# Moving a softplus series, splitting a recurrence around a product, and leaving the last chunk of four output tiles to the end

## The reference

```python
z = x @ w_in                               # 8 x 512 mixer columns, then 4 x 1024 gate columns
# A: RG-LRU
a_conv = causal_dwconv(rg_buf, a_x, rg_conv_w) + rg_conv_b
r = sigmoid(a_conv @ w_a + b_a); i = sigmoid(a_conv @ w_x + b_x)
log_a = -8 * r * softplus(-lam)
a = exp(log_a); b = sqrt(-expm1(2 * log_a)) * (i * a_conv)
h_t = a_t * h_{t-1} + b_t                  # scan over the tokens
y_a = h * gelu(a_gate)
# B: conformer conv (31 taps) + LayerNorm; C: trailing means; D: short gated conv
merged = sum_n sigmoid(gates_n) * (branch_n @ w_branch[n])
x = LN(alpha * x + merged @ w_out)
x = LN(alpha * x + (silu(x @ w_gate) * (x @ w_up)) @ w_down)
```

## Time and profile before

| | |
|---|---|
| median of three executions | 1031.92 us |
| the profiled execution | 1031.38 us |
| its span, first to last instruction | 1029.6 us |
| PE busy | 973.7 us, 95% of the span |
| DVE busy | 495.5 us, 48% |
| POOL busy | 475.1 us, 46% |
| ACT busy | 315.8 us, 31% |
| mean granted TensorE clock | 0.977 of 2.4 GHz |

### The profile page before, as it was taken

One profiled execution on the slowest core, in us unless ns is written; L12 is line 12 of the kernel. 1 busy time (PEld: TensorE's weight loads), 2 busy tenths in 40 slices (PEclk: granted clock), 3 DMA queues, 4 the chain that ended last, 5 costly groups with the idle time before them and its releaser, 6 DMA issues.

```text
span 1029.6 us, 18839 instructions
## 1 busy us (share of the span) xinstructions
PE 973.7 (95%) x7622; PEld 967.7 (94%) x7622; DVE 495.5 (48%) x647; ACT 315.8 (31%) x445; POOL 475.1 (46%) x338
## 2 busy tenths in 40 slices
PE   6979999999999789999998999999999999999993
PEld 5979999999999789999998988999999999999993
DVE  2896979791107788453445683222232222101017
ACT  3413232227336122323233335222322222212121
POOL 3735465665273343444456367443343344344423
PEclk9989999999999898999999999999999999999997
DMA  8513332222323222233334212222322332323202
GB/s 231 151 49 91 96 97 81 81 73 71 92 65 91 62 63 80 71 92 92 90 105 123 63 42 81 83 81 85 98 81 84 99 122 72 97 73 97 73 1 87
DMA packets 166652, 89.28 MB, mean 87 GB/s; under 512 B 4634, under 2 KB 164674, under 8 KB 166609
## 3 DMA queue, kind: packets, MB, share of 16 engines
q1 hardware_dynamic: 164377, 87.75, 28.9%
q10 hardware_dynamic: 2232, 0.92, 0.3%
HBM read 85.49 MB, written 3.17 MB: 86 GB/s over the span
## 4 chain that ended last, share of the span: by engine, by line
PE 81%; DVE 11%; issue 2%; POOL 2%; SPq 2%; ACT 1%; DMA 1%; DVEq 0%; POOLq 0%
PE main L901 73%; PE main L1051 5%; DVE scr L1351 1%; POOL x_lo L556 1%; DVE scr L1357 1%; PE aux L888 1%; SPq L367 1%; DVE prod L1339 1%; DVE aux L1271 1%; PE aux L1051 1%; DMA ln_tok<-in_ln_b 1%; DVE spv L1201 1%; DVE scr L1350 1%; DVE scr L1364 1%; DVE y L1370 0%
## 5 line engine op out<-in xcount | busy, mean ns | idle before, releaser
L459 POOL TENSOR_TENSOR w_lo<-raw,w_hi 128x1024 fp32r<-128x1024 f32 (+1 forms) x168 | 375.4, 2237 | 497.1 <-ACT w_hi L600 494.8
L901 PE MATMUL main<-x_hi,w_lo 128*128 128x272 f32 x1664 | 346.7, 290 | 8.9 <-DVE dch_pad L1296 7.3
L901 PE MATMUL main<-x_lo,w_hi 128*128 128x272 f32 x1664 | 344.6, 289 | 0.0
L901 PE MATMUL main<-x_hi,w_hi 128*128 128x272 f32 x1664 | 343.8, 288 | 0.0
L901 PEld LDWEIGHTS main<-x_hi,w_lo 128*128 128x128 f32 x1664 | 261.9, 189 | 9.6 <-issue 7.5
L901 PEld LDWEIGHTS main<-x_lo,w_hi 128*128 128x128 f32 x1664 | 262.9, 189 | 0.0
L901 PEld LDWEIGHTS main<-x_hi,w_hi 128*128 128x128 f32 x1664 | 261.2, 189 | 0.0
L600 ACT ACTIVATE w_hi<-raw 128x1024 fp32r<-128x1024 f32 x168 | 177.5, 1057 | 264.4 <-PE main L901 258.4
L1499 DVE TENSOR_TENSOR scr<-main,scr 128x544 f32<-128x544 f32 x21 | 15.2, 725 | 167.3 <-PE main L901 157.8
L901 PE MATMUL main<-y,w_hi 128*128 128x272 f32 x512 | 87.8, 295 | 0.0
L901 PEld LDWEIGHTS main<-y,w_hi 128*128 128x128 f32 x512 | 75.3, 196 | 0.0
(11 more groups left out here) (286 smaller groups left out, 1077.4 us busy)
## 6 DMA issues: line engine op xcount, KB each, us to landing
raw<-in_w_in SPq DMA_DIRECT2D x64, 512.0 KB, 4.0
raw<-in_w_ff_gate SPq DMA_DIRECT2D x22, 512.0 KB, 3.8
raw<-in_w_ff_up SPq DMA_DIRECT2D x22, 512.0 KB, 3.8
raw<-in_w_branch SPq DMA_DIRECT2D x32, 256.0 KB, 3.3
raw<-in_w_ff_down SPq DMA_DIRECT2D x16, 512.0 KB, 3.5
raw<-in_w_out SPq DMA_DIRECT2D x8, 512.0 KB, 3.7
raw<-in_w_ff_down SPq DMA_DIRECT2D x8, 384.0 KB, 3.1
x_tok<-in_x_prompt SPq DMA_DIRECT2D x4, 512.0 KB, 6.9
```

Source lines behind the costliest of these rows:

```text
L459: pool.tensor_tensor(w_lo[s][:, 0:n, :], raw[s][:, 0:n, :], w_hi[s][:, 0:n, :].bitcast(F32), ALU.subtract).then_inc(w_lo_ready, 1)
L901: mm = pe.matmul(slot(ps_slot)[:, h, :], w[s][:, k, :], x[:, h * HALF:(h + 1) * HALF], start=(first and k == 0 and j == 0), stop=(last and ...
```

## The change

It has three parts.

1. The first three softplus operations move on DVE from the start into c = 3 of the input projection, behind the one that makes `Y_A` (L1320); the other 15 move behind `product(0, 0, 1)`. On ACT, the exponential moves from the start to just before `pairs(0, 0)`. A new semaphore `spv_ready` is waited for by ACT before the tanh (L765).
2. `recurrence` is cut in two: `decay_and_input` (L1350 to L1357) now runs before `product(1, i, 0)`, together with the waits for `sqrt_ready` and `gelu_ready`; the rest stays between the two products.
3. In the first half of the output projection, tiles 0 to 3 run chunks 0 to 6 only. After the fourth of them, PE waits for the last chunk of `merged` and runs it for the four tiles in turn, each signalling `half_done`.

```diff
@@ scalar
             for u in range(2, RING):
                 hi(u, u)
-            act.wait_ge(lam_ready, 1)
-            act.activation(spv[:, 1, :], spv[:, 0, :], ACT.Exp).then_inc(z_ready, 1)
             act.wait_ge(sm_landed, 5 * 16)
@@
+            act.wait_ge(lam_ready, 1)
+            act.activation(spv[:, 1, :], spv[:, 0, :], ACT.Exp).then_inc(z_ready, 1)
             pairs(0, 0, tails=True)
@@
             act.wait_ge(side_out, 3 * KW)
+            act.wait_ge(spv_ready, 1)
             for c in range(KW):
                 act.activation(th[:, c, :], th[:, c, :], ACT.Tanh, scale=spv[:, 7, c:c + 1])\
@@ tensor: half_unit gets k0=0, the number of its first chunk
-                for k, (xh, xl) in enumerate(xs):
+                for k, (xh, xl) in enumerate(xs, k0):
...
-                        mm = pe.matmul(bank, w[:, k, :], x[:, cols], start=(first and k == 0 and j == 0),
-                                       stop=(last and k == len(xs) - 1 and j == 2))
+                        mm = pe.matmul(bank, w[:, k, :], x[:, cols], start=(first and k == k0 and j == 0),
+                                       stop=(last and k == k0 + len(xs) - 1 and j == 2))
@@
-                    half_unit(*w, xs, main[:, step % 4, 0:HALF], h,
-                              ready=merged_ready if step == 0 else None)\
+                    if step < RING:
+                        half_unit(*w, xs[:KD - 1], main[:, step, 0:HALF], 0,
+                                  ready=merged_ready if step == 0 else None, last=False)
+                        if step == RING - 1:
+                            pe.wait_ge(merged_ready, KD)
+                            for j in range(RING):
+                                half_unit(w_hi[j], w_lo[j], xs[KD - 1:], main[:, j, 0:HALF], 0,
+                                          first=False, k0=KD - 1).then_inc(half_done, 1)
+                        continue
+                    half_unit(*w, xs, main[:, step % 4, 0:HALF], h)\
                         .then_inc((half_done, unit_done)[h], 1)
@@ vector
-            after(link(ve.tensor_scalar(spv[:, 2, :], lam, -1.0, None, ALU.mult)))
-            ve.tensor_tensor(spv[:, 0, :], lam, spv[:, 2, :], ALU.min).then_inc(lam_ready, 1)
-            after(link(ve.tensor_scalar(spv[:, 3, :], spv[:, 2, :], 0.0, None, ALU.max)))
-            ve.wait_ge(z_ready, 1)
...
-            after(link(ve.tensor_scalar(spv[:, 7, :], spv[:, 6, :], 4.0, None, ALU.mult)))
+            def lambda_parts():
...
+            def softplus():
+
+                ve.wait_ge(z_ready, 1)
...
+                ve.tensor_scalar(spv[:, 7, :], spv[:, 6, :], 4.0, None, ALU.mult).then_inc(spv_ready, 1)
@@ for c in range(KW)
                 ve.tensor_tensor(Y_A[:, c + KW, :], xc[:, c, :], Y_A[:, c, :].bitcast(F32), ALU.subtract)\
                   .then_inc(ax_used, 1)
+                if c == KW - 1:
+                    lambda_parts()
                 conformer_taps(c, range(CONF_TAPS_3, CF_TAPS), taps_done)
@@
-            def recurrence(c):
+            def decay_and_input(c):
...
+            def recurrence(c):
+
+                s_d, s_a, s_b, s_x = S
@@ q = 0
                 for mm in range(2):
                     product(0, i, mm)
+                if i == 0:
+                    softplus()
@@ q = 1
-                    product(q, i, 0)
                     if q == 1:
                         ve.wait_ge(sqrt_ready, 1)
                         ve.wait_ge(gelu_ready, 1)
+                        decay_and_input(i)
+                    product(q, i, 0)
+                    if q == 1:
                         recurrence(i)
                     product(q, i, 1)
```

More of the change, by code:

```diff
@@ L270, in build @@
         misc_ready, conf_ready = sem("misc_ready"), sem("conf_ready")
-        lam_ready, z_ready = sem("lam_ready"), sem("z_ready")
+        lam_ready, z_ready, spv_ready = sem("lam_ready"), sem("z_ready"), sem("spv_ready")
         raw_landed = [sem(f"raw_landed{s}") for s in range(RING)]
@@ L1042, in _, with half_unit @@
                     pairs(q, i, xs, branch_ready)
-            def half_unit(hi_w, lo_w, xs, bank, h, ready=None, n0=0, first=True, last=True):
+            def half_unit(hi_w, lo_w, xs, bank, h, ready=None, n0=0, first=True, last=True, k0=0):
                 cols = slice(h * HALF, (h + 1) * HALF)
-                for k, (xh, xl) in enumerate(xs):
+                for k, (xh, xl) in enumerate(xs, k0):
                     if ready:
@@ L1190, in _ @@
             lam = miscT[:, :, V_LAM:V_LAM + 1].rearrange("p c o -> p (c o)")
-            after(link(ve.tensor_scalar(spv[:, 2, :], lam, -1.0, None, ALU.mult)))
-            ve.tensor_tensor(spv[:, 0, :], lam, spv[:, 2, :], ALU.min).then_inc(lam_ready, 1)
-            after(link(ve.tensor_scalar(spv[:, 3, :], spv[:, 2, :], 0.0, None, ALU.max)))
-            ve.wait_ge(z_ready, 1)
-            after(link(ve.tensor_scalar(spv[:, 4, :], spv[:, 1, :], 2.0, None, ALU.add)))
-            after(link(ve.reciprocal(spv[:, 4, :], spv[:, 4, :])))
@@ L1197, in _ @@
[L1197 to L1201, removed]
-                                                   ALU.add, ALU.mult)))
@@ L1203, in _ @@
[L1203 to L1206, removed]
-            after(link(ve.tensor_scalar(spv[:, 7, :], spv[:, 6, :], 4.0, None, ALU.mult)))
+            def lambda_parts():
+                after(link(ve.tensor_scalar(spv[:, 2, :], lam, -1.0, None, ALU.mult)))
+                ve.tensor_tensor(spv[:, 0, :], lam, spv[:, 2, :], ALU.min).then_inc(lam_ready, 1)
+                after(link(ve.tensor_scalar(spv[:, 3, :], spv[:, 2, :], 0.0, None, ALU.max)))
@@ new lines, in softplus @@
+            def softplus():
+                ve.wait_ge(z_ready, 1)
+                after(link(ve.tensor_scalar(spv[:, 4, :], spv[:, 1, :], 2.0, None, ALU.add)))
+                after(link(ve.reciprocal(spv[:, 4, :], spv[:, 4, :])))
+                after(link(ve.tensor_tensor(spv[:, 4, :], spv[:, 4, :], spv[:, 1, :], ALU.mult)))
+                after(link(ve.tensor_tensor(spv[:, 5, :], spv[:, 4, :], spv[:, 4, :], ALU.mult)))
+                after(link(ve.tensor_scalar(spv[:, 6, :], spv[:, 5, :], 1.0 / 17, None, ALU.mult)))
+                for n in (15, 13, 11, 9, 7, 5, 3):
+                    after(link(ve.scalar_tensor_tensor(spv[:, 6, :], spv[:, 6, :], 1.0 / n, spv[:, 5, :],
+                                                       ALU.add, ALU.mult)))
+                after(link(ve.scalar_tensor_tensor(spv[:, 6, :], spv[:, 6, :], 1.0, spv[:, 4, :],
+                                                   ALU.add, ALU.mult)))
+                after(link(ve.scalar_tensor_tensor(spv[:, 6, :], spv[:, 6, :], 2.0, spv[:, 3, :],
+                                                   ALU.mult, ALU.add)))
+                ve.tensor_scalar(spv[:, 7, :], spv[:, 6, :], 4.0, None, ALU.mult).then_inc(spv_ready, 1)
```

## The result

The changed kernel takes 1010.07 us (median of 1005.98, 1009.45, 1010.68 and 1010.88), the kernel before 1032.37 us in the runs beside it. The ratio is 0.9769, 95% interval 0.9749 to 0.9789: 21.8 to 25.9 us, or 2.3%, faster. The profiled execution took 1009.45 us with a span of 1007.6, 22.0 us less than the span before. I had forecast 12.8 us. The direction was right, the size was not.

A forecast was written before the change was run, and what follows sets the result against it. PE bounds the kernel, busy 973.7 of 1029.6 us, so only its waits and slow-clock time can be won. -0.7 + 2.7 - 11.1 - 3.7 = -12.8 us, from 1031.92 to 1019.1; own range 1015 to 1023, with three rivals 1009.5 to 1027.

The forecast's parts named there:

- the four terms of the sum: Start stall -0.7 us, new wait at `packed` +2.7, recurrence -11.1, output tiles -3.7.
- the race: First decay of q = 1: POOL's `w_lo` starts 0.05 us ahead of DVE, which is held; gain 11.1 us.
- the wait of 5.9 us: First round of q = 1: PE waits 5.9 us for slot 1, then loses 2.2 in slow matmuls.
- a rival at 1012.5 us: First decay of q = 1: DVE gets ahead of POOL at 318.1, 6.6 us less; chance 0.12.
- Part 2, the later rounds: Rounds after the first in q = 1: PE waits only 0 to 0.6 us, too short to lower the clock.
- Part 1, the start: Start, PE's wait for L1296: the next DVE operations wait for POOL likewise; gain 0.7 us, slow clock stays.
- The fifth turn: Start: a fifth DVE operation, L1256 of c = 0, is held by POOL's next `w_lo` and ends at 47.8.
- Part 1, `packed`: End of input projection: the late exponential and a table load delay `packed`; PE loses 2.7 us, between 1.3 and 4.3.
- the bound of 1.3: PE's new wait at `packed`: the low end of 1.3 to 2.7 us.
- The 0.7 for the clock: Behind the new wait at `packed`: 0.7 us lost to slower matmuls, added to a wait of 2.0.
- Part 3: Output projection: the 3.3 us wait and 1.6 behind it go, 1.2 of new waits come; gain 3.7 us.
- one rival at a time: Rivals: start stall gone 1009.5 (0.14), DVE first 1012.5 (0.12), later rounds DVE-bound 1026.2 (0.10), every round held 1043 (0.04).

The follow-up runs named there:

- e2: The kernel before with only the recurrence split (decay and input ahead of the first product): 1013.88 us, ratio 0.9827.
- e3: The kernel before with only the change to the four output tiles: 1029.35 us, ratio 0.9966.
- e4: The kernel after with one 0.2 us DVE operation added between the statistics and the first decay: 1014.90 us, ratio 0.9839.
- e5: The kernel after with one 0.2 us DVE operation added ahead of the bias operation L1271 of c = 0: 1009.84 us, ratio 0.9795.
- e1: The kernel before with only the softplus moved, the exponential on ACT along with it: 1032.78 us, ratio 1.000.
- e8: The kernel after with `sm_lo` later, first three softplus operations and exponential back at the start, all four `wx_hi` ahead of the first square: 1000.28 us, ratio 0.9697.
- e6: The kernel after with POOL's `sm_lo` moved behind the `w_lo` of unit 8: 1002.58 us, ratio 0.9720.

## Why the prediction was right or wrong

By the profiles, the four terms of the sum were forecast as -0.7, +2.7, -11.1 and -3.7 us and came as -2.5 (1.5 against e2 and e3), +0.9, -17.6 and -2.8.

**Part 2, the race (11.1 us forecast, 17.9 measured alone).** This is the step that failed: the wait of 5.9 us with 2.2 of slow matmuls in the first round of q = 1, which came as a wait of 1.2 us with the clock at its upper level. The mechanism, the list of held operations and their prices were right, as e4 shows. Wrong was who comes first. I had read that POOL's `w_lo` starts 0.05 us before the statistics *end* (318.05 against 318.10), and let the first decay start after that end, and after the loop's entry. But on DVE an operation without a dependency follows before the one ahead of it has ended: L1367 starts 0.36 us after L1401, which lasts 0.44. Worked with starts, in the rows of before (317.65 and 0.36 against 318.05), DVE was ahead by 0.04 us. I had that outcome as a rival at 1012.5 us and gave it 0.12. A step that two rows decide by 0.05 us should have been given near to one half, and its 6.6 us should have set the bounds of the range.

**Part 2, the later rounds.** Right: no wait of PE in them. The second products came in time although L1386 and L1389 were held in the rounds 1 to 3 (1.96 and 1.41 us).

**Part 1, the start (0.7 forecast).** The reason was right: the softplus waited for POOL, its successors inherit it, the stall stays. The size was off twice, in opposite directions. The fifth turn (L1271) was not taken, as the turns before it were done some 0.65 us sooner than I had added up: it ended at 45.6 instead of 47.8. With 0.8 us lost again at the copy L1304 and the small differences before it, PE started at 55.30 instead of 57.48, 2.2 us sooner than before for the 0.7 forecast. But behind it more of the slow stretch was left than in e2, e3 and e5. What part 1 gained there, at the end of unit 5, is 1.5 us (e1 against e2 and e3).

The Trainium skill (SBUF — State Buffer, Who interferes with whom) had the filter taps, with one SBUF input, free of POOL; the trace agrees, the ten of them last 6.67 us in both kernels. In the same section the Trainium skill says that whoever issues first gets the shared port pair for the whole instruction. The traces agree: in e4 a DVE operation 0.55 us behind POOL lasts 2.16 us, in the kernel after the same one, 0.04 us ahead, 0.44.

**Part 1, `packed` (2.7 forecast, 0.9 measured).** The chain of steps was right, its sizes were taken too high. `lam_ready` came 0.4 us ahead of even the early end that I had counted: its operation ran ahead of POOL's window (0.16 us at 229.13), 0.3 us behind the end of `Y_A`'s, where I had 0.7. So the wait was 0.7 us, below the bound of 1.3, and I had taken 2.0 from the middle of the bounds. The 0.7 for the clock did not come: the granted clock is 1.00 from 230 to 238 us. The Trainium skill (ScalarE: Activation LUTs, What ACT_TABLE_LOAD costs) has about 1380 ns of draining beside the load. The trace does not agree: the load lasts 1.28 us and the sigmoid starts 1.30 us after the load does. With the draining the loss would have been 1.4 us more, an estimate from that figure.

**Part 3 (3.7 forecast, 3.5 measured, 2.8 in the profiles).** Right, with 1.3 us of new waits for 1.2 forecast. The profile shows less, 2.8 of 3.7. The three waits for `wx_lo` are what I had worked out, but e8, which removes them, is 2.0 us faster in this stretch, 0.7 more than their 1.3. The clock is at its upper level in both. A likely reason is that each new start of PE costs some 0.2 us beyond the wait listed for it, which counts from the end of a matmul of 0.29 us where in a stream the next one starts 0.125 after its start; no run isolates it. I had given it nothing. The remaining tenths I can't resolve.

**The range.** 1009.5 to 1027 for a median of 1010.07; by the ratio, which takes the before of each call, the kernel after stands at 1008.1 on the base I started from, just outside. The range reached only as far as one rival at a time, and the smaller costs were each priced at the dear side, with 2.7 us for `packed` the dearest.

Open are the place and the length of the slow stretch at the start, and the last tenths of part 3.

## What to carry to other kernels

Work that is taken off an engine in front of a stall gains little (here nothing that whole times show) if it was mostly waiting for another engine's operations that will hold its successors as well: look at how long the same operation takes elsewhere, and move the other engine's work instead (e6). Where engine A's next operation and engine B's come within some tenths of a microsecond, compare their starts, not an end with a start, treat the order as open, and put the whole price of both orders in the range. A moved step should be priced with what it brings along, here a table load (a second one fell into ACT's idle time) and a wait that stood in front of everything else on ACT.

## What the runs showed of the hardware

- DVE and POOL take turns operation by operation: four DVE operations in a row, which take 0.18 to 1.20 us alone, lasted 2.4 to 3.3 us, each beside one POOL operation (kernel after, 32.37 to 44.13).
- On DVE an operation without a dependency started 0.36 us after the start of one that lasts 0.44 us (kernel after, 316.10 and 316.46).
- One DVE operation of 0.20 us, at the wrong place, cost a wait of 5.6 instead of 1.2 us on PE, and 6.5 us in its stretch (e4). At another place it made DVE 2.2 us late and the end of unit 5 0.4 us (e5).
- The time lost at the lower clock did not grow with the wait at the start: 2.2 to 2.9 us after four waits of 5.0 us, 1.5 after waits of 6.5 and 7.2 us, 3.0 after 7.3 us in the kernel before. The clock was low for 6.8 us in seven profiles and for 10.2 in that of the kernel before.
- A wait of PE of 0.7, 1.0 or 1.2 us (`packed` and the product in the kernel after, `dch_pad` in e6) lowered no clock.
- A load of an activation table took 1.28 us, and the activation started 1.30 us after the load did. A load in front of an activation that waits for a semaphore ran before the wait was over (224.61, the activation at 229.33).
